# Recurrent stage of a hybrid decoder: a new order of ScalarE's and VectorE's instructions around the roots, the scans and the last z tile

## The reference, cut to what matters

```python
y = b + sum(xp[:, j:j + L] * w[j] for j in range(CONV_W))            # conv of 4 taps
r = sigmoid(xc_blocks @ w_r + b_r);  i = sigmoid(xc_blocks @ w_i + b_i)
log_a = -LRU_C * r * softplus(-lam);  a = exp(log_a)
bterm = sqrt(-expm1(2.0 * log_a)) * (i * xf)
h_t = a_t * h_{t-1} + bterm_t                                        # scan over tokens
o_b = h * silu(z_b)
```

## Time and profile before

| | us |
|---|---|
| median of 3 runs | 1997.71 |
| lowest and highest run | 1996.53 and 1999.6 |
| the profiled execution, own time | 1998.1 |
| its span in the profile | 1996.3 |
| TensorE busy (share of span) | 1960.0 (98%) |
| VectorE busy | 1166.1 (58%) |
| ScalarE busy | 727.0 (36%) |
| GpSimd busy | 239.5 (12%) |

### The profile page before, as it was taken

One profiled execution on the slowest core, in us unless ns is written; L12 is line 12 of the kernel. 1 busy time (PEld: TensorE's weight loads), 2 busy tenths in 40 slices (PEclk: granted clock), 3 DMA queues, 4 the chain that ended last, 5 costly groups with the idle time before them and its releaser, 6 DMA issues.

```text
span 1996.3 us, 32098 instructions
## 1 busy us (share of the span) xinstructions
PE 1960.0 (98%) x13224; PEld 1825.1 (91%) x13224; DVE 1166.1 (58%) x1997; ACT 727.0 (36%) x1112; POOL 239.5 (12%) x360
## 2 busy tenths in 40 slices
PE   8999999999999999999999999999999999999997
PEld 7789888898899999999988988988988999999997
DVE  7665555565566777424486545646556667753345
ACT  4321222222236766422333222222122366754222
POOL 1011110120232200000001201202102322000000
PEclk9999999999999999999999999999999999999999
DMA  6434523543343333322245334434433533332222
GB/s 209 129 111 159 179 102 125 167 157 104 140 147 97 104 103 102 118 75 75 96 165 173 111 127 150 166 108 142 159 120 122 165 100 99 97 126 81 84 78 79
DMA packets 105567, 247.04 MB, mean 124 GB/s; under 512 B 10798, under 2 KB 51230, under 8 KB 105038
## 3 DMA queue, kind: packets, MB, share of 16 engines
q1 hardware_dynamic: 78446, 149.78, 24.0%
q0 software_dynamic: 26976, 95.22, 14.2%
HBM read 186.07 MB, written 49.18 MB: 118 GB/s over the span
## 4 chain that ended last, share of the span: by engine, by line
PE 80%; DVE 8%; ACT 5%; DMA 2%; issue 2%; ACTq 1%; DVEq 1%; SPq 0%
PE bank L1507 19%; PE bank L1509 19%; PE bank L1508 19%; PE bank L1570 5%; PE bank L1571 5%; PE bank L1572 5%; DMA w_raw<-in_w_units 2%; DVE w_lo L419 2%; PE last L1586 1%; PE last L1570 1%; PE last L1572 1%; PE last L1571 1%; ACT w_hi L411 1%; PE sums L1601 1%; DVE ct L1302 1%
## 5 line engine op out<-in xcount | busy, mean ns | idle before, releaser
L1507 PE MATMUL bank<-xn_hi,w_hi 128*128 128x296 f32 x2432 | 729.5, 300 | 2.7 <-DVE vtok_lo L1128 2.5
L1509 PE MATMUL bank<-xn_lo,w_hi 128*128 128x296 f32 x2432 | 726.7, 299 | 0.0
L1508 PE MATMUL bank<-xn_hi,w_lo 128*128 128x296 f32 x2432 | 723.3, 297 | 0.0
L1507 PEld LDWEIGHTS bank<-xn_hi,w_hi 128*128 128x128 f32 x2432 | 457.1, 188 | 11.0 <-issue 6.6
L1508 PEld LDWEIGHTS bank<-xn_hi,w_lo 128*128 128x128 f32 x2432 | 458.3, 188 | 0.1
L1509 PEld LDWEIGHTS bank<-xn_lo,w_hi 128*128 128x128 f32 x2432 | 456.1, 188 | 0.0
L419 DVE TENSOR_TENSOR w_lo<-w_raw,w_hi 128x1024 fp32r<-128x1024 f32 x245 | 299.0, 1223 | 203.6 <-ACT w_hi L411 196.2
L411 ACT ACTIVATE w_hi<-w_raw 128x1024 fp32r<-128x1024 f32 x245 | 258.7, 1056 | 380.3 <-DMA w_raw<-in_w_units 376.0
L1507 PE MATMUL bank<-oa_hi,w_hi 128*128 128x296 f32 x512 | 154.5, 302 | 0.0
L1509 PE MATMUL bank<-oa_lo,w_hi 128*128 128x296 f32 x512 | 153.3, 299 | 0.0
L1508 PE MATMUL bank<-oa_hi,w_lo 128*128 128x296 f32 x512 | 152.5, 298 | 0.0
(11 more groups left out here) (258 smaller groups left out, 3048.1 us busy)
## 6 DMA issues: line engine op xcount, KB each, us to landing
w_raw<-in_w_units SPq DMA_DIRECT2D x216, 512.0 KB, 3.5
S<-in_state_ret POOLq DMA_DIRECT2D x64, 512.0 KB, 5.0
out_ret_s<-S POOLq DMA_DIRECT2D x64, 512.0 KB, 5.9
w_raw<-in_w_units SPq DMA_DIRECT2D x64, 256.0 KB, 3.2
vst<-v_scr SPq DMA_DIRECT2D x8, 512.0 KB, 4.1
out_ret_p<-Sp POOLq DMA_DIRECT2D x8, 512.0 KB, 4.0
v_scr<-vtok_hi SPq DMA_DIRECT2D x16, 160.0 KB
dec<-in_decay POOLq DMA_DIRECT2D x9, 264.0 KB, 3.2
```

The lines of the kernel that those rows point to most:

```text
L1507: pe.matmul(ps, w_hi[:, slot, cols], x_hi, start=first, stop=False)
L1508: pe.matmul(ps, w_lo[:, slot, cols], x_hi, start=False, stop=False)
L1509: return pe.matmul(ps, w_hi[:, slot, cols], x_lo, start=False, stop=last)
```

## The change

No instruction is added or removed; only the order on ScalarE and VectorE changes.

ScalarE: `xb(…, 1)` of a group moves from its start to the group before. `xb(next, 0)` now stands ahead of that group's Exp and Tanh, and `xb(next, 1)` ahead of its Sqrt. In the last group the first GA tile takes the first place, and the second GA tile with a weight split takes the second. `gates(0)` moves ahead of `high_xc(2)`, and the first half of z tile 2 is read between them.

VectorE: the products L1339 become a function `raised`, which runs behind the next group's first `conv`. The second `conv` and a weight split go ahead of the scan of tile 0; `low_xc(0)` follows that scan. The scan of tile 2 and the `silu` of tile 1 go ahead of the third `conv` and its `low_xc`. The `silu` of tile 2 goes ahead of one of the two weight splits that stood before it.

```diff
@@ -796,13 +796,14 @@
                     apart(act)
                     act.activation(xc_hi[:, t, :], xc[:, t, :], ACT.Copy).then_inc(xch_ready, 1)
 
-                def tanh_zl(it, g, t):
+                def tanh_zl(it, g, t, which=(0, 1)):
 
                     gg = l * GROUPS + it * 2 + g
-                    if gg >= 1:
+                    if gg >= 1 and 0 in which:
                         act.wait_ge(ob_ready, (gg - 1) * 3 + t + 1)
                         apart(act)
-                    for n, (a, b) in enumerate(HALVES):
+                    for n in which:
+                        a, b = HALVES[n]
                         name = (("proj", g, 3 + t), n)
                         wait_job(act, "L", l, it, name)
                         act.activation(zl[:, t, a:b], psum_of("L", name)[:, 0:HALF], ACT.Tanh, scale=0.5)\
@@ -844,10 +845,10 @@
 
                 xb(0, 0, 0)
                 split_hi(act, "L", l, 0, 0)
+                xb(0, 0, 1)
                 for it in range(0, 2):
                     for g in range(2):
                         gg = l * GROUPS + it * 2 + g
-                        xb(it, g, 1)
                         split_hi(act, "L", l, it, g * 6 + 1)
                         act.wait_ge(gw_in[g], (l * 2 + it + 1) * 16 * len(GATE_RECTS))
                         act.activation(gw_hi[:, :, :], gw[:, g, :, :], ACT.Copy).then_inc(gwh_ready, 1)
@@ -860,9 +861,10 @@
                         split_hi(act, "L", l, it, g * 6 + 3)
                         tanh_zl(it, g, 1)
                         split_hi(act, "L", l, it, g * 6 + 4)
+                        gates(it, g, 0)
+                        tanh_zl(it, g, 2, (0,))
                         high_xc(gg, 2)
-                        gates(it, g, 0)
-                        tanh_zl(it, g, 2)
+                        tanh_zl(it, g, 2, (1,))
                         split_hi(act, "L", l, it, g * 6 + 5)
                         gates(it, g, 1)
                         act.drain().then_inc(i_ready, 1)
@@ -873,15 +875,21 @@
                         act.sem_inc(gw_free, 1)
                         act.wait_ge(par_ready, l + 1)
                         apart(act)
+                        last = (it, g) == (1, 1)
+                        if last:
+                            tanh_g("GA", 0, 0)
+                        else:
+                            xb(it + g, 1 - g, 0)
                         for t in range(3):
                             act.activation(aa[:, t, :], rr[:, t, :], ACT.Exp, scale=lam_nc[:, ds(it * 6 + (g * 3 + t), 1)])
                             act.drain()
                             act.activation(rr[:, t, :], rr[:, t, :], ACT.Tanh, scale=lam_c[:, ds(it * 6 + (g * 3 + t), 1)])\
                                .then_inc(at_ready, 1)
-                        if (it, g) != (1, 1):
-                            xb(it + g, 1 - g, 0)
+                        if last:
+                            tanh_g("GA", 0, 1)
+                            split_hi(act, "GA", l, 0, 1)
                         else:
-                            tanh_g("GA", 0, 0)
+                            xb(it + g, 1 - g, 1)
                         act.drain()
                         for t in range(3):
                             act.activation(rr[:, t, :], rr[:, t, :], ACT.Sqrt).then_inc(sqrt_ready, 1)
@@ -893,7 +901,7 @@
                             act.activation(ob_hi[:, k, :], ob[:, k, :], ACT.Copy).then_inc(obh_ready, 1)
                     for it in range(0, 2):
                         for i in range(4):
-                            if (ph, it, i) != ("GA", 0, 0):
+                            if (ph, it, i) not in (("GA", 0, 0), ("GA", 0, 1)):
                                 tanh_g(ph, it, i)
                                 split_hi(act, ph, l, it, i)
                 done = 0
@@ -1333,6 +1341,10 @@
                         dve.tensor_tensor(ii[:, t, :], ii[:, t, :], xc[:, t, :], MUL)
                         if t == 0:
                             split_lo(dve, "L", l, it, g * 6 + 6)
+
+                def raised(it, g):
+
+                    gg = l * GROUPS + it * 2 + g
                     for t in range(3):
                         dve.drain()
                         dve.wait_ge(at_ready, gg * 3 + (t + 1))
@@ -1368,10 +1380,12 @@
                         last = None if (it, g) == (0, 0) else (it - 1 + g, 1 - g)
                         conv(it, g, 0)
                         if last:
+                            raised(*last)
+                        conv(it, g, 1)
+                        split_lo(dve, "L", l, it, g * 6 + 1)
+                        if last:
                             scan(*last, 0)
                         low_xc(gg, 0)
-                        conv(it, g, 1)
-                        split_lo(dve, "L", l, it, g * 6 + 1)
                         low_xc(gg, 1)
                         dve.wait_ge(gwh_ready, gg + 1)
                         dve.tensor_tensor(gw_lo[:, :, :], gw[:, g, :, :], gw_hi[:, :, :].bitcast(f32), SUB)\
@@ -1380,16 +1394,17 @@
                             scan(*last, 1)
                         split_lo(dve, "L", l, it, g * 6 + 2)
                         silu(it, g, 0)
-                        conv(it, g, 2)
-                        low_xc(gg, 2)
                         if last:
                             scan(*last, 2)
                         silu(it, g, 1)
+                        conv(it, g, 2)
+                        low_xc(gg, 2)
                         split_lo(dve, "L", l, it, g * 6 + 3)
+                        silu(it, g, 2)
                         split_lo(dve, "L", l, it, g * 6 + 4)
-                        silu(it, g, 2)
                         split_lo(dve, "L", l, it, g * 6 + 5)
                         inputs(it, g)
+                raised(1, 1)
                 scan(1, 1, 0)
                 scan(1, 1, 1)
                 split_lo(dve, "GA", l, 0, 1)
```

## The result

The changed kernel takes 2006.82 us (median of 6 runs, 2002.98 to 2007.61) against 1998.3 us of the kernel before beside it (6 runs): a ratio of 1.004, 95% interval 1.0027 to 1.0053. It is slower by 8.5 us. The forecast was no change at 1998.9 us, and the time lies above the range's upper end of 2004.3. The profiled execution took 2006.67 us, with a span of 2004.9, 8.6 more than before.

The account below looks back on a forecast made before the run. TensorE's holes in six recurrent groups were taken as the bound, blamed on the z product. A copy wait replacing that wait gave +1.2 us on the profiled 1998.1, or 1998.9 against the 1997.7 median: no change; range 1993.0 to 2004.3.

Parts of the forecast that it names:

- What bounds the kernel: Recurrent stage: TensorE's holes in six groups of 47.45 us, about 1.55 us lost each, blamed on the z product.
- The z tile 2 product goes ahead of one split: VectorE's end of six groups: moving this product before one weight split alone gives back 1.14 us per group.
- The list from R to R + 44.2: From TensorE's start of gates(2) to the next group's last mix copy issue: the engines' work adds to 44.2 us.
- 44.25 + L: Length of each of six groups as a closed loop including the copy's landing, replacing 47.45 us; even at 3.2 us.
- The order of load and copy: Before gates(2) in six groups: the weight load leaves about 1.3 us ahead of the last mix copy.
- The landing L: Last mix copy, issue to landing: taken as 3.4 us, bounds 2.5 and 4.7; gives +1.2 us over six groups.
- replaced by another of its size: Forecast's own case: z wait gives way to a similar copy wait, landing between 2.6 and 3.8 us; chance 0.57.
- B: Copy queues behind the weight load at gates(2), landing 4.0 to 4.7 us: +4.8 to +9 us; chance 0.22.
- A: Last mix copy lands undisturbed in 2.5 us or less: groups of 46.75 us, -4.2 us, 1993.5; chance 0.18.
- A's second bound: If the loop is also 0.3 us shorter, ScalarE's sigmoid chain bounds: 46.5 us per group, -5.5 us, 1992.2.
- C: Recurrent stage's end late by 1 us or more per layer behind the last group's third scan: 2001; chance 0.03 for tipping.
- First groups, small parts: First group of each layer: copy leaves some 3 us before needed, so effect 0, and the sigmoid wait stays.

Follow-up runs that it names:

- the filled kernel: Changed kernel with 12 extra matmuls ahead of TensorE's wait for the last mix copy in six groups; 2007.0 us, ratio 1.0039.

## Why the prediction was wrong

**What bounds the kernel: half right.** TensorE's holes in six groups, 47.45 us each, were the right sum. But I took the hole for the z product's and gave the two splits ahead of it the blame. "The z tile 2 product goes ahead of one split ... that alone gives 1.14 us back per group" is refuted: it gives 0.01 us. The later experiments point to a loop through ScalarE with a split on it, worth 0.9 us a group where it was moved. A wait of TensorE for VectorE is not proof that VectorE's last instruction is what to move.

**The list from R to R + 44.2: right.** Taking the start of the second group's loop at 621.78 less the gate matmuls' 1.6, 620.2, the list puts `w_hi` of the split at its end at 641.1, and it ended at 639.91 + 1.04 = 640.95; the copy's issue was due at 664.4 and was at 664.19. VectorE's wait for `w_hi` was 1.00, as forecast. ScalarE's for tile 0 was 0.86 at this place, about the 1 us forecast; behind the third groups it was 1.5 and 2.1, and behind the second ones, where TensorE was slow, 3.4 and 4.4 for both halves. With the measured landings 44.25 + L gives 6 x 44.25 + 23.1 = 288.6 us for the six groups, and for the kernel with the load held 265.5 + 15.5 = 281.0 against 281.71 measured. The form of the loop held, and with it its break-even at 3.2.

**The order of load and copy: right.** I put the load 1.3 us ahead; it was 1.37 to 2.00.

**The landing L: the step that failed first.** I took 3.4, near a lone row of 3.6, and gave values from 3.9 up a chance of 0.22. The runs showed 3.85 on the mean, with three of six at 3.9 or more, and 4.7 as the highest, which is the bound from the earlier trace rows. That row was the nearest by mechanism (a copy beside a load), and I leaned on one that was nearest by name. The copy of 3.6 us was slow for another reason. The DMA view of the kernel before, from its issue to its landing (709.00 to 712.60), lists one packet of a queue that the other seven copies do not have:

```profile
q8 instruction: 1, 0.02, 2.1%
```

The profile calls q8 an instruction queue. In the kernel before and in the seven experiments where no load leaves between 3.3 us ahead of the copy and 2.4 behind it, 64 copies in all, ten took 3.4 to 4.1 us, and each of the ten has a packet of q8 between issue and landing; the other 54 took 2.4 to 2.9 and none has one. So this row said nothing about a load. The term is 6 x 0.45 = 2.7 us too small.

The DMA page of the Trainium skill ("DMA: Bandwidth & Descriptors", Queues, rings and completion order) has the engines take turns between queues with work, and I noted that by it the copy would be nearer the upper bound. The runs agree with it in sign: 2.5 us alone, 4.0 to 5.8 right behind a load. The estimate of 2.3 us for the lone copy, from the fit of the same page (Anatomy of one DMA), is near the 2.5 measured.

**The missing term: the clock, the larger part.** The forecast for the six groups was 6 x 47.65 = 285.9 us; 293.6 was measured, 7.7 more, of which the landings are 2.7. Measured 293.6, by the loop with the measured landings 288.6. Of the 5.0 us between, about 41 matmul starts stand 0.245 us apart instead of 0.136, 4.5 us. The loop begins with these matmuls, so what they lose goes into it: the next copy left some 1.9 us later behind a slow stretch than behind none. With the waits filled the loop's formula gives 6 x 44.25 + 24.3 = 289.8 and 291.2 was measured, 1.4 us over instead of 5.0. I had one wait "replaced by another of its size" and gave nothing to what TensorE's clock might do behind longer ones. The changed kernel's own runs point the same way: five had a mean granted clock of 0.996 or 0.997 and took 2006.1 to 2007.6 us, and the sixth had 0.999 and took 2002.98, inside my range. That is one run, and sooner landings would show the same. Removing the slow stretches did not bring this time back: the filled kernel's rest was 2.7 us longer.

**Rivals.** B was the place (the copy behind the load, at `gates(2)` in six groups), and its price of 4.8 to 9 us holds the measured 8.5, but not by its own terms: landings gave 288.6 - 284.7 = 3.9 of it, which is under B, and the rest is the clock. A's landing is what holding the load brings; its 1993.5 came out as 1996.0 against 1998.2. A's second bound, 46.5 us a group, was passed with the split moved: 46.3. C did not come: `w_lo` shows no wait behind the recurrent stage. **First groups, small parts:** the first group takes 46.77 us in layer 0 and 46.5 in layer 1, before and after alike, and one of their copies landed in 4.1 us with nobody waiting.

**The range** ended at 2004.3, since it left out the upper half of B. A landing of 3.85 alone lies inside it (3.9 us over before); with the 5.0 us that came on top the forecast leaves it.

**What stays open:** the part of the 5.3 us by which the span outside the six groups differs between these kernels that the slow stretch at the start of layer 1 leaves over; why filling the waits won no time; why the clock falls behind one wait and not behind a longer one; and whether moving ScalarE's split alone would do in the kernel before what it did with the third conv ahead of the scan. The spread of L in the changed kernel is not open: the copies that left 1.37 and 1.38 us behind their load took 4.5 and 4.7, those at 1.70 to 1.74 took 3.4 to 3.9, and the one at 2.00 took 3.0.

## What to carry to other kernels

When an edit moves a small copy to the end of a chain, look up which large transfer leaves in the 2 us before it, and price the copy from a row that has such a neighbour; if it is late, hold the load rather than hurry the copy. Before giving a wait to the last instruction in front of it, ask whether another engine's chain comes due within a microsecond, and move one thing alone to see. Look at the spacing of the matmuls behind a wait as well as at the wait: a slower TensorE there counts into any loop that starts with these matmuls.

## What the hardware showed that I had not expected

- A copy of 148 KB by GpSimd's queue lands in 2.4 to 2.9 us alone and also when a load leaves 2.4 us or more behind it (54 of 64 copies). Behind a load of 512 KB it takes 4.0 to 5.8 us at a distance of 0.5 us, 4.6 to 5.7 at 0.6 to 1.3, and 3.0 to 4.7 at 1.4 to 2.0. Its arrival is 4.5 to 6.4 us after the load's issue in all of these.
- One packet of the instruction queue q8 during such a copy goes with a landing of 3.4 to 4.1 us, in ten of ten cases without a load near. The 5.8 us above had one too; the seven others at that distance took 4.0 to 4.7 without.
- The load pays too: 3.8 to 5.0 us in the changed kernel against 3.5 on the median of all.
- With a load 0.85 us behind the copy (first groups of the changed kernel) it landed once in 2.5 us and once, with a packet of q8, in 4.1.
- TensorE's granted clock fell behind three of six waits for the copy, for some 3.4 us each: about 14 matmuls at 0.245 us, some 1.5 us lost each time. The length of the wait alone does not sort them: it fell behind 1.38 us and not behind 1.91. It fell at the start of layer 1 too, in seven of twelve kernels.
